# Low parts of the mixers' weight tiles moved from VectorE to GpSimd, the centring moved ahead of the pooling sums, and x fetched in four pieces

## The reference, cut to what matters

```python
shift1, scale1, gate1, shift2, scale2, gate2 = mod        # silu(cond) @ w_mod + b_mod
h = _rmsnorm(x, norm1_g) * (1 + scale1) + shift1
u = h @ w_in
q, k, v, p_in, c_in, g_in = _split_in(u)
y_a = attention(q, k, v, ...) @ w_oa                      # neighbourhood / context attention, 8 heads x 64
y_b = _pool_mixer(p_in, w_pool, pool_scale) @ w_ob        # centred mean windows 2/4/8/16, minus token
y_c = _conv_mixer(c_in, ...) @ w_oc                       # a * sigmoid(g), depthwise conv of 31 taps, LayerNorm, silu
gates = sigmoid(g_in + b_gate)                            # three branches
merged = gates[0] * y_a + gates[1] * y_b + gates[2] * y_c
x = x + gate1 * (merged @ w_out)
h2 = _rmsnorm(x, norm2_g) * (1 + scale2) + shift2
a, b = split(h2 @ w_gu)
x = x + gate2 * ((silu(a) * b) @ w_down)
return final_rmsnorm(x)
```

## Time and profile before

| what | value |
|---|---|
| runs | 2087.10, 2082.64, 2085.36 us; median 2085.36 |
| profiled execution | 2082.74 us |
| its span, first to last instruction | 2080.9 us |
| mean granted TensorE clock | 0.987 |
| busy: TensorE, VectorE, ScalarE, GpSimd | 2000.7, 952.3, 607.6, 558.3 us |
| attention block begins (first load) / rear block begins | 364.95 / 846.6 us |
| one tap on VectorE | 1.48 us |
| TensorE on one projected tile i without a wait | 13.8 us (905.1 to 918.9) |
| TensorE done with projected tile i = 1 | 919.1 us |
| gates transfer, 768 KB, issue to landing | 5.9 us (median) |
| gates sigmoid (L1776), 512 tokens | 1.49 us |
| mixing of a chunk of 512 tokens on VectorE, nothing beside it | 3.3 us (911.9 to 915.2) |
| upper part, 512 tokens (L1781) / low part of the total (L1905) | 0.63 / 1.54 us |
| silu of the convolution's rows ends (L609) | 326.9 us |

### The profile page before, as it was taken

How to read it: one execution, slowest core, us unless ns; L and a number is a source line. 1 busy time by engine, 2 the same in 40 slices (tenths; PEclk the granted TensorE clock), 3 DMA queues, 4 the chain that set the end, 5 groups by cost and what they waited for, 6 DMA issues and landing times.

```text
span 2080.9 us, 26410 instructions
## 1 busy us (share of the span) xinstructions
PE 2000.7 (96%) x10768; PEld 1754.2 (84%) x10768; DVE 952.3 (46%) x1712; ACT 607.6 (29%) x1093; POOL 558.3 (27%) x392
## 2 busy tenths in 40 slices
PE   8999898998999999899899999999999999999998
PEld 3899787898899999788787888888888888888887
DVE  5699953355556665256415651312303213123035
ACT  3512222455555555343313211111111111111113
POOL 0000000444334443134442232232222322322225
PEclk9999999999999999999999999999999999999999
DMA  8552333633344332545510221101111111111112
GB/s 306 187 151 68 105 132 124 145 91 100 89 97 106 91 87 63 194 139 183 189 51 10 72 81 51 41 31 41 41 41 40 32 41 41 41 31 41 41 41 102
DMA packets 198775, 185.19 MB, mean 89 GB/s; under 512 B 33664, under 2 KB 174208, under 8 KB 197632
## 3 DMA queue, kind: packets, MB, share of 16 engines
q1 hardware_dynamic: 198656, 183.52, 29.2%
HBM read 142.60 MB, written 40.89 MB: 88 GB/s over the span
## 4 chain that ended last, share of the span: by engine, by line
PE 47%; DVE 4%; DMA 4%; POOL 2%; issue 1%; ACT 1%; SPq 0%; DVEq 0%; ACTq 0%; POOLq 0%
PE ps_all L144 46%; DMA branch_and_gates<-gates 2%; DVE branch_and_gates L1975 1%; DMA branch_and_gates<-branch_dram 1%; POOL w_lo L1900 1%; DVE branch_and_gates L1978 1%; DVE normed L2011 1%; DVE normed L2017 1%; DMA gates<-last_gates 1%; POOL AL L1905 1%; DVE AL L2023 0%; DMA XT<-xT_dram 0%; ACT branch_and_gates L1776 0%; ACT w_hi L1757 0%; PE ps_all L1680 0%
## 5 line engine op out<-in xcount | busy, mean ns | idle before, releaser
L144 PE MATMUL ps_all<-AH,w_hi 128*128 128x512 f32 (+3 forms) x2112 | 767.3, 363 | 33.7 <-PEq L229 7.4
L144 PE MATMUL ps_all<-AL,w_hi 128*128 128x512 f32 (+3 forms) x2112 | 755.7, 358 | 0.0
L144 PE MATMUL ps_all<-AH,w_lo 128*128 128x512 f32 (+3 forms) x2112 | 755.0, 357 | 0.0
L144 PEld LDWEIGHTS ps_all<-AH,w_hi 128*128 128x128 f32 x2112 | 403.1, 191 | 78.3 <-issue 22.9
L144 PEld LDWEIGHTS ps_all<-AH,w_lo 128*128 128x128 f32 x2112 | 402.4, 191 | 42.1
L144 PEld LDWEIGHTS ps_all<-AL,w_hi 128*128 128x128 f32 x2112 | 403.6, 191 | 39.0
L1900 POOL TENSOR_TENSOR w_lo<-w_raw,w_hi 128x1024 fp32r<-128x1024 f32 x78 | 190.6, 2444 | 574.1 <-ACT w_hi L1757 574.1
L1988 DVE SCALAR_TENSOR_TENSOR XT<-ps_all,mod,XT 128x512 f32<-128x512 f32 (+1 forms) x288 | 187.0, 661 | 208.8 <-PE ps_all L144 194.4
L2039 DVE TENSOR_TENSOR hidden<-ps_all,silu_a 128x512 f32<-128x512 f32 (+1 forms) x66 | 39.8, 602 | 501.8 <-PE ps_all L144 501.6
L144 PE MATMUL ps_all<-actH,w_hi 128*128 128x512 f32 (+1 forms) x528 | 188.1, 356 | 0.0
L144 PE MATMUL ps_all<-actL,w_hi 128*128 128x512 f32 (+1 forms) x528 | 187.7, 355 | 0.0
(11 more groups left out here) (172 smaller groups left out, 2555.7 us busy)
## 6 DMA issues: line engine op xcount, KB each, us to landing
w_raw<-w_gu_dram SPq DMA_DIRECT2D x44, 512.0 KB
w_raw<-w_in_dram SPq DMA_DIRECT2D x42, 512.0 KB
wmod_then_mixers<-w_mod_dram SPq DMA_DIRECT2D x20, 1024.0 KB, 8.7
branch_and_gates<-gates SPq DMA_DIRECT2D x16, 768.0 KB, 5.9
w_raw<-w_down_dram SPq DMA_DIRECT2D x22, 512.0 KB
gates<-gate_rows SPq DMA_DIRECT2D x42, 224.0 KB, 1.9
kq_src<-kT_dram SPq DMA_DIRECT2D x16, 384.0 KB, 6.0
xT_dram<-xT_then_mixers SPq DMA_DIRECT2D x1, 5120.0 KB, 17.1
```

The costliest lines, as they stand in the source:

```text
L144: mm = nc.tensor.matmul(out, w, a[:, k, cols[0]:cols[1]], start=(first and part == 0), stop=(last and part == 2))
```

## The change

In the front, VectorE's seventeen `lower` of units 2 to 18 are taken out of its program and made by GpSimd, each as soon as its upper part is there. VectorE's taps follow one another without anything between, `centre` comes directly behind them and `windows` behind it. The four stores of the convolution's rows are issued ahead of the last q rows' store.

In the rear, the weight tile of two output tiles ahead is split behind chunk 3i + 1 instead of 3i + 2, ahead of opening the next gates. The two sums of `mix` are written as scalar_tensor_tensor with a factor of 1.0. x comes back in four transfers of 1.25 MB, one before and three between the loads of w_out's tiles 3 to 5. The first two weight tiles of the feed-forward part are split at m = 3 and 6 of the second pass instead of 4 and 6, the upper parts of the norm are made in two groups of eight, and VectorE adds the residuals of m = 3 to 5 between the norms of chunks 0 and 2. The banks of `rb` get a semaphore of their own, because their order among VectorE's jobs changes.

```diff
@@ -321,11 +321,12 @@
                             sp.dma_start(g.d["branch"][4 + t, :, :], ppad[:, t, 0:T]).then_inc(branch_stored, 16)
+                    if u == 17:
+                        for t in range(2):
+                            for part, (a, b, at) in enumerate(((0, LAT, 0), (LAT, T, CCTX))):
+                                sp.wait_ge(silu_ready, 2 * t + part + 1)
+                                sp.dma_start(g.d["branch"][6 + t, :, a:b], conv[:, t, at:at + b - a]).then_inc(branch_stored, 16)
                 store_rows(MIX - 1)
-                for t in range(2):
-                    for part, (a, b, at) in enumerate(((0, LAT, 0), (LAT, T, CCTX))):
-                        sp.wait_ge(silu_ready, 2 * t + part + 1)
-                        sp.dma_start(g.d["branch"][6 + t, :, a:b], conv[:, t, at:at + b - a]).then_inc(branch_stored, 16)
                 sp.wait_ge(ck_stored, 16)
@@ -746,38 +747,23 @@
                 modulation(0)
-                lower(2)
                 glu_out(0)
-                lower(3)
                 modulation(1)
                 modulation(2)
-                lower(4)
                 modulation(3)
...
                 glu_out(1)
-                lower(5)
                 modulation(5)
...
                 dve.wait_ge(zeroed, 2)
-                for u in range(4, U_MEAN):
-                    taps(5 * (u - 4), 5 * (u - 4) + 3)
-                    lower(u + 2)
-                    taps(5 * (u - 4) + 3, 5 * (u - 3))
+                taps(0, CONV_K)
+                centre()
                 windows()
-                lower(13)
-                centre()
                 modulation(6)
                 modulation(7)
-                lower(14)
                 normalise()
-                lower(15)
-                modulation(8)
-                modulation(9)
-                lower(16)
-                modulation(10)
-                modulation(11)
-                lower(17)
-                lower(18)
+                for n in range(8, NG):
+                    modulation(n)
                 late_mod()
@@ -788,6 +774,9 @@
                 nc.gpsimd.memset(wp[:, :, :], 0.0).then_inc(zeroed, 1)
+                for u in range(2, MIX + 1):
+                    pool.wait_ge(W.hi_ready, u + 1)
+                    nc.gpsimd.tensor_tensor(W.lo[:, u % 2, :], W.raw[:, :], W.hi[:, u % 2, :].bitcast(F32), ALU.subtract).then_inc(W.lo_ready, 1)
@@ -1335,7 +1324,7 @@
 REAR_AT = {job: n for n, job in enumerate(REAR)}
-CONSUMER = {"gate": "act", "a": "act", "mod": "act", "stat": "stat", "fstat": "stat"}
+CONSUMER = {"gate": "act", "rb": "rb", "a": "act", "mod": "act", "stat": "stat", "fstat": "stat"}
@@ -1419,10 +1408,11 @@
         done, a_free, d_free, s_free = sem("rear_done"), sem("rear_free_act"), sem("rear_free_dve"), sem("rear_free_stat")
+        rb_free = sem("rear_free_rstd")
         b_in, b_hi, b_lo = [sem(f"branch_in{b}") for b in range(3)], sem("branch_hi"), sem("branch_lo")
...
         step, mixed, m_hi, m_lo = sem("merge_step"), sem("chunk_mixed"), sem("m_hi"), sem("m_lo")
-        x_in = (sem("x_back0"), sem("x_back1"))
+        x_in = [sem(f"x_back{n}") for n in range(4)]
         zeroed, squared, added = sem("sum_zeroed"), sem("squared"), sem("square_added")
@@ -1446,7 +1436,7 @@
             n = REAR_AT[job]
-            return {"act": a_free, "dve": d_free, "stat": s_free}[consumer(job)], RELEASED[n]
+            return {"act": a_free, "dve": d_free, "stat": s_free, "rb": rb_free}[consumer(job)], RELEASED[n]
@@ -1522,6 +1512,9 @@
+                def load_rows(n):
+                    sp.dma_start(XT[:, 2 * n:2 * n + 2, :], g.d["xT"][2 * n:2 * n + 2, :, :].rearrange("k p t -> p k t")).then_inc(x_in[n], 16)
+
                 def load_gate2(n):
@@ -1556,10 +1549,11 @@
                 sp.wait_ge(*finished(("proj", KD - 1, 2, 2)))
-                for half in range(2):
-                    sp.dma_start(XT[:, 4 * half:4 * half + 4, :], g.d["xT"][4 * half:4 * half + 4, :, :].rearrange("k p t -> p k t")).then_inc(x_in[half], 16)
+                load_rows(0)
                 for u in range(UNITS_WO + 3, UNITS_FFN + len(FFN)):
                     load_w(u)
+                    if u < UNITS_WO + 6:
+                        load_rows(u - UNITS_WO - 2)
                     if u in (UNITS_FFN + 2, UNITS_FFN + 3, UNITS_FFN + 4, UNITS_FFN + 5):
@@ -1846,10 +1840,10 @@
                     upper(q)
+                    if q % 3 == 1:
+                        split(GATES + 2 + q // 3)
                     if q + 2 < MERGED:
                         open_gates(q + 2)
-                    if q % 3 == 2:
-                        split(GATES + 2 + q // 3)
                 for m in range(KD):
@@ -1858,11 +1852,10 @@
                         roots(("stat", 0), 0, 6)
-                    if m == 3:
-                        for n in range(2 * KD):
-                            normed_upper(n)
-                    if m in (4, 6):
-                        split(UNITS_FFN + (m - 4) // 2)
+                    if m in (3, 6):
+                        split(UNITS_FFN + (m - 3) // 3)
+                        for n in range(KD):
+                            normed_upper((m - 3) // 3 * KD + n)
                     square(m, 1)
@@ -1942,8 +1935,8 @@
                 for m in range(KD):
-                    if m in (4, 6):
-                        lower(UNITS_FFN + (m - 4) // 2)
+                    if m in (3, 6):
+                        lower(UNITS_FFN + (m - 3) // 3)
                     if m < KD - 1:
@@ -1975,11 +1968,11 @@
                             dve.wait_ge(*released(job))
-                            nc.vector.tensor_tensor(x[1], x[1], x[2], ALU.add).then_inc(step, 1)
+                            nc.vector.scalar_tensor_tensor(x[1], x[1], 1.0, x[2], ALU.mult, ALU.add).then_inc(step, 1)
                         if j == 2:
...
                             dve.wait_ge(step, q + 1)
-                            nc.vector.tensor_tensor(x[0], x[0], x[1], ALU.add).then_inc(mixed, 1)
+                            nc.vector.scalar_tensor_tensor(x[0], x[0], 1.0, x[1], ALU.mult, ALU.add).then_inc(mixed, 1)
@@ -2009,7 +2002,7 @@
                         mm = nc.vector.tensor_tensor(normed[:, n % 3, 0:b - a], XT[:, f, a:b], bank_of(job)[:, 0:b - a], ALU.mult)
-                        mm.then_inc(d_free if f == KD - 1 else scaled, 1)
+                        mm.then_inc(rb_free if f == KD - 1 else scaled, 1)
                         if f == KD - 1:
@@ -2071,8 +2064,8 @@
                 for m in range(KD):
-                    if m % 4 == 0:
-                        dve.wait_ge(x_in[m // 4], 16)
+                    if m % 2 == 0:
+                        dve.wait_ge(x_in[m // 2], 16)
                     for c in FIRST_PASS:
@@ -2080,8 +2073,10 @@
                 normalise(0)
+                for m in range(3, 6):
+                    residual(("wo", m, 1), m, 1, 2)
                 normalise(2)
-                for m in range(3, KD):
+                for m in range(6, KD):
                     residual(("wo", m, 1), m, 1, 2)
```

## The result

| | before | after |
|---|---|---|
| median (lowest to highest) | 2086.23 us (2082.64 to 2087.60), 4 runs | 2128.61 us (2124.98 to 2133.39), 4 runs |
| profiled execution, its span | 2082.74, 2080.9 us | 2124.98, 2123.2 us |
| ratio, 95% interval | | 1.021, 1.018 to 1.023 |

The change costs 42 us. The forecast was 2051 us, faster with a chance of 0.85; what came is rival A, at the earliest of its places.

A forecast was written before the change was run, and what follows sets the result against it. TensorE works in 96% of the span, so only its waits and the low clock after them can be won. Terms of 5.5, 5.1, 3.0, 7.3, 8.3 and 4.7 sum to 33.9 us: 2051 us, range 2041 to 2072.

The forecast's parts named there:

- rival A: Front: GpSimd is held out of the taps, so TensorE waits for a low part; middle value 2097 us, chance 0.13.
- Part 1: Front mixers: low parts move to GpSimd; collisions cost VectorE 2.25 us each among the taps, which grow by about 6.7 us.
- part 6: Front taps, in rival A: low part 6 locked out to the end of the run, TensorE stands about 77 us.
- Taps and gated product: Front, VectorE: taps run from about 135 to 239 us, and the second gated product comes at 127.4.
- Part 2: Front: centring ahead of the pooling sums removes the 6.8 us wait and 1.6 us of low clock; 5.5 us gained.
- unit 17: Front: its low part, made on GpSimd, is ready 10 us early; 3.4 + 1.7 = 5.1 us gained.
- Covered with little to spare: Front: pooling sums, late next after the centring, come just in time for TensorE; without that cover up to 4 us.
- Part 3: End of the front, SP queue: convolution-row stores issued earlier leave one store of 0.62 MB at the end; 3.0 us gained.
- Parts 4 and 5: Rear: splitting merge weights one chunk earlier gains 7.3 us; x in four pieces around w_out's tiles gains 8.3 us.
- Rival B: Rear: the gates loop keeps holding TensorE, with some of part 6's second-norm work left undone; 2061 us, chance 0.17.
- Part 6: Rear, second norm: earlier weight splits and residuals cut waits and low clock around the second token sum; 4.7 us gained.
- The sum: Whole kernel: the terms' gains add to 33.9 us, giving a forecast of 2051 us against the median.

The follow-up runs named there:

- experiment 2: The kernel after, with a memset of 16 columns behind each pair of taps, 31 in all: 2051.31 us in one run, beside 2083.53 for before.
- experiment 3: The kernel after, with one single memset of 16 columns, behind tap pair 15: 2105.8 us in one run, beside 2081.42 for before.
- experiment 1: The kernel after, but each tap waits for the tap directly before it, not the one two before: 2064.26 us, ratio 0.991 to before.
- experiment 5: The kernel after, but low parts of units 2 to 12 back on VectorE at their old places: 2046.35 us, ratio 0.983 to before.
- experiment 4: The kernel after, with memsets behind each pair of taps and every second pair of modulation products: 2050.22 us, ratio 0.986 to before.
- experiment 7: The kernel before, with one edit, centring ahead of the pooling sums: 2079.35 us, ratio 0.9987 to before.
- experiment 6: As experiment 5, but unit 2's low part also left on GpSimd: 2046.32 us, ratio 0.983 to before.

## Why the prediction was wrong, by its own steps

- **Part 1, the step that failed**: "the two exclude each other, and a low part inside the taps costs VectorE 2.15 us", taken as 2.25 each with a handover after one tap at most. Excluding each other was right. The handover was not: in the taps of the change VectorE paid nothing and GpSimd stood 87.14 us. The 2.15 us are the price only where GpSimd is let in, as in all seven requests of experiment 2 and in one of three in experiment 3. The evidence was in the earlier trace rows: one request of four or five, at 1193.12, was held to the end of its run. The sentence of the Trainium skill that I weighed ("SBUF — State Buffer", section "Who interferes with whom"), that whoever starts first holds the port for the whole instruction, agrees with the exclusion, 5.20 for 3.05 us in experiment 2. By it GpSimd would have had its turn at the end of one tap; it waited over the ends of some 57, and the measurement decides.
- **Rival A** had mechanism and size: part 6 held to the end of the taps, 77 us in its list; 73.8 measured. That 2051 + 77 = 2128 is also the time that came is luck: the hold of unit 4, 11.1 us with its clock, was not in it, and without the two holds the change would stand near 2042, not 2051. The chance of 0.13 did not follow from my own count. Parts 6 to 9, four requests, would each have decided by themselves; if one in four or five is held, none of four is held with 0.78^4 = 0.37, so rival A should have stood at about 0.6, as the likeliest. Its list of waits has an error of its own: it falls by 12.5 us a part, though it puts the requests 15 us apart, and in experiment 1 they are 14.0 to 15.4 apart. From the 73.8 measured, the list is 74, 59, 45, 29 and 14 us, and parts 6 to 8 alone exceed the gain of 35; then one of them is held with 1 - 0.78^3, about 0.5. I had asked how often a request is held, not how often one of a chain of costly ones is. That count also came from the rear's gate products, and in the front a far larger share was held, as told below. The second hold, of unit 4 in the modulation products (9.0 us and 2.1 of clock), was in no case: I had priced that place at 4.5 us for two collisions.
- **Taps and gated product**: forecast end 239 us and the product at 127.4; measured 231.15 and 124.20, since no collision took place.
- **Part 2 and unit 17** (5.5 + 5.1): with the holds gone they are worth 13.2 us in experiment 5, where the taps carry no collisions of GpSimd, and 8.8 in experiment 4, where they do; the forecast of 10.6 lies between. "Covered with little to spare" was right for the pooling sums, but what gives way is not the sums themselves: it is the low part behind them (experiment 7).
- **Part 3**: forecast 3.0, measured 3.3. SP's queue after, which answers to the earlier trace rows:

```profile
427.87 0.32 SPq L261 DMA_DIRECT2D qT_dram<-xT_then_mixers  x1
431.36 1.09 SPq L912 DMA_DIRECT2D kq_src<-kT_dram  x2
```

- **Parts 4 and 5**: their sum was forecast as 15.6 and came as 18.1, but the halves were cut wrongly. The 8.3 us were given to x in four pieces alone; the early split removes most of the same wait, so beside it the pieces are worth the 1.4 us of a wait and nothing that the median shows. Rival B, the gates loop, did not hold: 0.4 us of waits in the whole merge, and no more than 2.7 in the other profiles with this rear.
- **Part 6**: 4.7 forecast, 5.4 measured (179.4 to 174.0); the token sums wait 1.1 us instead of 2.8.
- **The sum**, 33.9 us, lies between what comes out where no hold costs TensorE time: experiment 4 gains 31.2 against its chip's runs of before, experiment 5 gains 37.2. The second is the best version here, together with experiment 6: 2046.3 us, faster than both kernels.

What stays open is what decides a single request. Amid plain taps, the requests at 146.20 (after) and 145.52 and 207.17 (experiment 3) were held and the one at 193.35 was not. Nor does the form of the instruction decide: in the kernel after, the front's modulation products held all three parts that were asked for with several products still to come (4.81, 17.77 and, at 383.01, 8.26 us), while the rear's gate products (L2045), of the same form, shape and waits, let three of four in at once, and the fourth took 5.63 us:

```profile
1219.15 2.45 POOL L1893 TENSOR_TENSOR w_lo<-w_raw,w_hi 128x1024 fp32r<-128x1024 f32 x1 [0.48 <-ACT w_hi L1751]
1234.07 5.63 POOL L1893 TENSOR_TENSOR w_lo<-w_raw,w_hi 128x1024 fp32r<-128x1024 f32 x1 [12.48 <-ACT w_hi L1751]
```

No run here tells these apart.

## What to carry to other kernels

Work that reads SBUF on GpSimd should not be given a due time inside a run of VectorE instructions with two SBUF inputs that start one behind the other. A wait for the instruction before last, as the taps here have, is no opening. Price the work by the end of that run, although some requests are let in sooner, or put an opening in (a memset of 0.07 us was enough). And when two edits each remove the cause that is latest at the same wait, undo each singly before giving either its price.

## What the runs showed of the hardware that was not expected

- A GpSimd subtraction of 2.4 us lasted 87.14, 42.92, 29.86 and 17.77 us beside VectorE's scalar_tensor_tensor, while VectorE kept its 1.48 us a tap: the exclusion can be all to one side.
- A memset of 0.07 us (but not a pair of tensor_scalar) or a wait for the directly preceding instruction was enough to turn it: 2.4 to 3.8 us for GpSimd, 2.0 to 2.15 us for VectorE. Which property of the memset does it, no run shows.
- Each hold ended at the end of the run or at the memset, and the part 2.2 to 2.3 us later (126.49, 188.44, 233.34 us; in experiment 3 also 237.03 behind taps that ended at 234.83), so the span that the profile gives to such an instruction is nearly all waiting.
